# Delta rule of a two-block model: inverse as two 64x64 diagonal tiles per product, its levels in one stretch

## What is computed

```
decay = jnp.exp(jnp.where(causal, gc[..., :, None] - gc[..., None, :], -jnp.inf))
a_low = jnp.where(strict, jnp.einsum("bhnid,bhnjd->bhnij", k_beta, k) * decay, 0.0)
t_mat = a_low + jnp.eye(L, dtype=f32)
sol = lax.linalg.triangular_solve(t_mat, rhs, left_side=True, lower=True, unit_diagonal=True)
...
v_new = u_i - jnp.einsum("bhld,bhde->bhle", w_i, state)
```

## Time and profile before

| | us |
|---|---|
| median of 3 runs (917.66 to 919.14) | 919.08 |
| the profiled execution, its own time | 919.58 |
| its span, first to last instruction | 917.8 |
| TensorE busy | 904.7 |
| VectorE busy | 601.0 |
| ScalarE busy | 518.4 |

### The profile page before, as it was taken

One profiled execution on the slowest core, in us unless ns is written; L12 is line 12 of the kernel. 1 busy time (PEld: TensorE's weight loads), 2 busy tenths in 40 slices (PEclk: granted clock), 3 DMA queues, 4 the chain that ended last, 5 costly groups with the idle time before them and its releaser, 6 DMA issues.

```text
span 917.8 us, 16932 instructions
## 1 busy us (share of the span) xinstructions
PE 904.7 (99%) x6586; PEld 841.4 (92%) x6586; DVE 601.0 (65%) x959; ACT 518.4 (56%) x905; POOL 24.5 (3%) x36
## 2 busy tenths in 40 slices
PE   9999999999999999999999999999999999999998
PEld 7978899999998999999999999999987999999986
DVE  4689755555557666668786877755758455554576
ACT  6478754444446765567456464735549444444463
POOL 4100300000000000000000000000000000000000
PEclk9999999999999999999999999999999999999999
DMA  9814766665554455453222141415555555556541
GB/s 286 274 58 129 165 204 192 192 191 184 184 184 135 144 178 162 159 176 118 75 92 93 49 135 32 152 47 184 184 195 173 196 183 184 181 189 196 177 171 46
DMA packets 107647, 143.43 MB, mean 156 GB/s; under 512 B 3016, under 2 KB 95432, under 8 KB 107600
## 3 DMA queue, kind: packets, MB, share of 16 engines
q1 hardware_dynamic: 105648, 137.60, 46.6%
q0 software_dynamic: 1744, 4.98, 2.6%
q10 hardware_dynamic: 208, 0.20, 0.1%
HBM read 141.72 MB, written 1.05 MB: 156 GB/s over the span
## 4 chain that ended last, share of the span: by engine, by line
PE 82%; DVE 9%; ACT 5%; issue 3%; DMA 0%; DVEq 0%; ACTq 0%
PE ps L1762 15%; PE ps L1764 15%; PE ps L1763 15%; PE ps L1770 8%; PE ps L1768 8%; PE ps L1769 8%; PE ps L2170 2%; PE ps L2157 2%; PE ps L2174 2%; DVE R L1501 2%; DVE wl L1172 1%; ACT wh L627 1%; PE ps L1859 1%; PE ps L1841 1%; ACT R L951 1%
## 5 line engine op out<-in xcount | busy, mean ns | idle before, releaser
L1172 DVE TENSOR_TENSOR wl<-w_raw,wh 128x1024 fp32r<-128x1024 f32 x251 | 305.0, 1224 | 213.5 <-ACT wh L627 212.9
L1762 PE MATMUL ps<-xTh,wh 128*128 128x256 f32 (+1 forms) x1160 | 334.8, 289 | 0.9 <-DVE xTl L1198 0.8
L1763 PE MATMUL ps<-xTl,wh 128*128 128x256 f32 (+1 forms) x1160 | 326.2, 281 | 0.0
L1764 PE MATMUL ps<-xTh,wl 128*128 128x256 f32 (+1 forms) x1160 | 326.2, 281 | 0.0
L627 ACT ACTIVATE wh<-w_raw 128x1024 fp32r<-128x1024 f32 x251 | 263.1, 1053 | 81.5 <-PE ps L1770 60.2
L1762 PEld LDWEIGHTS ps<-xTh,wh 128*128 128x128 f32 x1160 | 219.1, 189 | 4.4 <-issue 2.7
L1763 PEld LDWEIGHTS ps<-xTl,wh 128*128 128x128 f32 x1160 | 218.4, 188 | 1.9 <-issue 1.0
L1764 PEld LDWEIGHTS ps<-xTh,wl 128*128 128x128 f32 x1160 | 219.2, 189 | 0.0
L1768 PE MATMUL ps<-wh,y 128*128 128x512 f32 x224 | 87.9, 392 | 0.0
L1770 PE MATMUL ps<-wh,y 128*128 128x512 f32 x224 | 87.6, 391 | 0.0
L1769 PE MATMUL ps<-wl,y 128*128 128x512 f32 x224 | 87.1, 389 | 0.0
(11 more groups left out here) (371 smaller groups left out, 1335.7 us busy)
## 6 DMA issues: line engine op xcount, KB each, us to landing
w_raw<-in_w_in_dram SPq DMA_DIRECT2D x42, 1024.0 KB, 5.2
w_raw<-in_w_ff_dram SPq DMA_DIRECT2D x32, 1024.0 KB, 5.5
w_raw<-in_w_ffn_gate_dram SPq DMA_DIRECT2D x11, 1024.0 KB, 5.3
w_raw<-in_w_ffn_up_dram SPq DMA_DIRECT2D x11, 1024.0 KB, 5.3
w_raw<-in_w_ffn_down_dram SPq DMA_DIRECT2D x11, 1024.0 KB, 4.9
w_raw<-in_w_out_dram SPq DMA_DIRECT2D x8, 1024.0 KB, 5.0
w_raw<-in_w_proj_a_dram SPq DMA_DIRECT2D x4, 1024.0 KB, 5.2
w_raw<-in_w_proj_b_dram SPq DMA_DIRECT2D x4, 1024.0 KB, 5.1
```

The source lines that it names most:

```text
L1172: TT(low_part, raw_unit(SLOT[p], j, layout), high_part.bitcast(F32), ALU.subtract).then_inc(w_lo, 1)
L1762: mm(out, wh_, xh, start=first, stop=False)
L1763: mm(out, wh_, xl, start=False, stop=False)
L1764: return mm(out, wl_, xh, start=False, stop=last)
```

## The change

**Compact form.** Levels 1 to 5 never leave the two diagonal blocks of 64 tokens, so `X_`, `XT_` and `PM_` are kept as 128 partitions x 64 columns (`Xc`, `XTc`, `PM_`), and each product of two 128x128 matrices becomes two products of 64x64, one on partitions 0 to 63 and one on 64 to 127. Level 6 is one 64x64 product per matrix in each of its two stages. The full `XT_` is put together afterwards by two ScalarE copies and one subtraction. The product for `X_` now goes to other PSUM banks (`fm`), with a semaphore of its own, and is issued after the one for `XT_` in each group. The transposition of `X_` is now made by 64x64 products with the identity, and VectorE copies it out (before: ScalarE).

**One stretch.** The levels stand in stages 6 to 17, with no steps between. `prepare`, `exponents`, `g_rows` come ahead of them, `out_transposes` behind, `out_root` in stage 3; `out_row` and `gate_rows` stay between the levels on VectorE. The silu of `zr` moves to the last stage. In stage 1 ScalarE's copy and split for unit 0 now both come after the norms.

**Besides.** The recurrent gate of the first block is computed with full 128x128 block-diagonal weights (before: two 64x64 halves each). The table of constants is smaller, some semaphores are merged, and TensorE's two middle rounds are written out (before: a loop).

```diff
-GDN_WEAVE = [9, 8, 4, 6, 4] + [1] * 12 + [4, 3, 3, 11]
+GDN_WEAVE = [2, 8, 4, 8, 7, 3] + [0] * 12 + [4, 3, 3, 22]
...
                         for j in range(2):
-                            last = mm(acc[:, 3 * g, j * P:(j + 1) * P], A_[:, 2 * g + j, :], XT_[:, 2 * g + j, :], start=True, stop=True)
+                            pr, out = 2 * g + j, acc[:, 3 * g, j * HB:(j + 1) * HB]
+                            if lv < 6:
+                                for part in blocks:
+                                    last = mm(out[part], A_[part, pr, part], XTc[part, pr, :], start=True, stop=True)
+                            else:
+                                last = mm(out[0:HB], A_[HB:P, pr, 0:HB], XTc[HB:P, pr, :], start=True, stop=True)
                         last.then_inc(lv_p[g], 1)
...
                         for j in range(2):
-                            pr = 2 * g + j
-                            last = mm(acc[:, 1 + g, j * P:(j + 1) * P], X_[:, pr, :], PM_[:, pr, :], start=True, stop=True)
+                            pr, out = 2 * g + j, acc[:, 1 + g, j * HB:(j + 1) * HB]
+                            for part in blocks[0:2 if lv < 6 else 1]:
+                                last = mm(out[part], Xc[part, pr, :], PM_[part, pr, :], start=True, stop=True)
+                        last.then_inc(lv_zt[g], 1)
...
                         if lv < 6:
                             for j in range(2):
-                                pr = 2 * g + j
-                                last = mm(acc[:, 1 + g, (2 + j) * P:(3 + j) * P], PM_[:, pr, :], X_[:, pr, :], start=True, stop=True)
-                        last.then_inc(lv_z[g], 1)
+                                pr, out = 2 * g + j, fm[:, g, j * HB:(j + 1) * HB]
+                                for part in blocks:
+                                    last = mm(out[part], PM_[part, pr, :], Xc[part, pr, :], start=True, stop=True)
+                            last.then_inc(lv_zx[g], 1)
...
-                for gate, w in ((fm[:, m % 2, 0:T1], wa_bd), (acc[:, m, 0:T1], wx_bd)):
-                    for half in (slice(0, 64), slice(64, 128)):
-                        last = mm(gate[half, :], w[half, m, half], xc[half, m, :], start=True, stop=True)
-                last.then_inc(r_ps, 1)
+                mm(fm[:, m % 2, 0:T1], wa_bd[:, m, :], xc[:, m, :], start=True, stop=True)
+                mm(acc[:, m, 0:T1], wx_bd[:, m, :], xc[:, m, :], start=True, stop=True).then_inc(r_ps, 1)
```

More of the change, by code:

```diff
@@ L69, in constant_table @@
     c[:, C_MLOW:C_LEV] = np.where(k < r, 0.0, NEG)
-    for n in range(LEVELS):
+    r64, k64 = np.arange(HB)[:, None], np.arange(HB)[None, :]
+    for n in range(LEVELS - 1):
         b = 1 << n
[L72 to L77, removed]
+        low = (r64 // (2 * b) == k64 // (2 * b)) & (r64 % (2 * b) >= b) & (k64 % (2 * b) < b)
+        c[:, level_mask(n)] = np.tile(low.T if n else low[:, 0::2], (2, 1))
+    c[:, C_ID2:C_MOBA] = np.tile(np.eye(HB, dtype=np.float32), (2, 1))
     diag = np.where(k <= r, 0.0, NEG)
@@ L960, in gdn_stage @@
                     ins.then_inc(kv_out, 1)
+                    if not (isinstance(a, int) and a == 0):
+                        out_root(a - 1)
                 if s == 4:
[L962 to L963 removed]
                     act.wait_ge(vT_ps, a + 1)
@@ L1023, in pair_round @@
                 before = ch.n
-                later = weave is GDN_WEAVE
                 for s, done in enumerate(finished(weave)):
                     stage(s, a)
-                    if later and s == 1:
-                        hi(fu + 4, 8, a)
                     for c in done:
-                        unit(c, fu + c, 8, a, pair, not (later and c == 0))
+                        unit(c, fu + c, 8, a, pair)
                 return ch.n - before if isinstance(ch.n, int) else None
@@ L1532, in gdn_stage @@
                     dve.wait_ge(inv_start, a + 1)
[L1533 to L1536, removed]
+                    low = PM_.rearrange("p r n -> p (r n)")[:, 0:4 * 32]
+                    first = cst[:, level_mask(0)].unsqueeze(1).to_broadcast([P, 4, 32])
+                    evens = A_.rearrange("p r (q two) -> p r q two", two=2)
+                    for b in range(2):
+                        part, qs = slice(HB * b, HB * b + HB), slice(32 * b, 32 * b + 32)
+                        ins = TT(rows4(low)[part], evens[part, :, qs, 0], first[part], ALU.mult)
+                    link(ins)
+                    grow(Xc, 0, 0, low.rearrange("p (m b) -> p m b", b=1)).then_inc(x0_out, 1)
                 if s == 4:
@@ L1545, in gdn_stage @@
                     prepare(a + 1)
-                if s == 10 and not (isinstance(a, int) and a == PAIRS - 1):
+                if s == 5 and not (isinstance(a, int) and a == PAIRS - 1):
                     exponents(a + 1)
-                if 5 <= s < 17 and s % 2 == 1:
-                    lv = (s - 5) // 2 + 1
+                if 6 <= s < 18 and s % 2 == 0:
+                    lv = (s - 6) // 2 + 1
+                    if lv == 1:
+                        for g in range(2):
+                            dve.wait_ge(xt0_ps, a * 2 + (g + 1))
+                            dve.tensor_copy(XTc[:, 2 * g:2 * g + 2, :], pairs(acc[:, 1 + 2 * g, 0:P])).then_inc(xt0_out, 1)
@@ L1557, in gdn_stage @@
+                    if not (isinstance(a, int) and a == 0):
+                        if 2 <= lv < 6:
+                            out_row(a - 1, lv - 2)
+                        elif lv == 6:
+                            gate_rows(a - 1)
+                if 6 <= s < 18 and s % 2 == 1:
+                    lv = (s - 6) // 2 + 1
                     for g in range(2):
-                        dve.wait_ge(lv_z[g], a * 6 + lv)
-                        z = acc[:, 1 + g, :].rearrange("p (r n) -> p r n", r=4)
@@ L1564, in gdn_stage @@
+                if s == 18 and not (isinstance(a, int) and a == 0):
+                    out_lo(a - 1)
+                if s == 18:
                     dve.wait_ge(uw_ps, a + 1)
@@ L1649, in _ @@
                 if m == 1:
-                    out_rows(3)
+                    for pr in range(4):
+                        out_row(3, pr)
+                    gate_rows(3)
                 if m == 4:
@@ L2133, in gdn_stage @@
                 if s == 4:
-                    pe.wait_ge(x0_out, a + 1)
-                    for pr in range(4):
-                        last = pe.transpose(acc[:, 3, pr * P:(pr + 1) * P], X_[:, pr, :], ident)
-                    last.then_inc(xt0_ps, 1)
                     pe.wait_ge(silu_v, a + 1)
@@ L2206, in gdn_stage @@
                     last.then_inc(o_ps, 1)
-                if s == 9 and not (isinstance(a, int) and a == PAIRS - 1):
-                    pe.wait_ge(tok_out, a + (PAIRS + 1))
-                    g_rows(a + 1)
-                if s == 13 and not (isinstance(a, int) and a == 0):
-                    pe.wait_ge(tok_out, a + (PAIRS + 1))
-                    pe.wait_ge(vb_out, a + 1)
-                    out_transposes(a - 1)
             def g_rows(b):
@@ L2251, in _ @@
             pair_round(GDN_WEAVE, gdn_stage, "fffffftt", G + 8, 0)
-            for i in rounds(pe, 2):
+            for i in range(2):
                 pair_round(GDN_WEAVE, gdn_stage, "fffffftt", G + 8, i + 1)
```

156 lines of the change are left out of this document (93 added, 63 removed).

## The result

The changed kernel takes **914.12 us** (median of 7 runs, 912.44 to 915.8) where the one before takes 919.17 beside it (7 runs, 917.66 to 919.76). The ratio is 0.9943, 95% interval 0.9932 to 0.9955, so it is faster by 0.6%. The profiled execution took 914.48 with a span of 912.7; before it was 919.58.

The account below looks back on a forecast made before the run. TensorE's work was taken to bound the kernel. Terms including -12.4 us (levels) and +9.8 (turn of a round) summed to -4.2: 915.4 in the profiled execution's time, so 914.9 us; range 908 to 928.

Parts of the forecast that it names:

- The pass: Spacing of 64-column passes on TensorE in the levels: 0.034 us taken, 0.028 if halves overlap, 0.066 as upper bound.
- A level: One of levels 1 to 5 of the inverse: 2.05 us, against 2.67 before without its steps.
- the first term: Levels 1 to 5 over four rounds: 20 x (2.05 - 2.67) = -12.4 us.
- Rival 3: TensorE-VectorE hand-overs in the levels priced too low eat the gain: about 918 to 920 us, chance 0.18.
- The turn: Before each round's sums of squares, seven steps no longer cover the wait for ScalarE: +2.46 x 4 = +9.8 us.
- Rival 2: The turn of a round costs nothing, something other than ScalarE's order sets the sums' start: 905.1 us, chance 0.08.
- rival 4: TensorE's clock falls to 1.2 GHz after each turn's 2.8 us wait: +14 us, so 929, chance 0.06.
- g_rows: Products ahead of the levels wait for prepare, late behind out_root: about 0.3 us in two rounds, +0.6 us.
- Entering and leaving the small form: Switching TensorE into and out of 64x64 products: about 0.1 us each time, +0.8 us in all.
- Level 6 and the transposition: The inverse's last level about 2.07 us, -1.4 in the sum; 16 small transposing passes plus VectorE's copy 0.91 us, +0.8.
- Recurrent gate: First block's gate: 16 full passes of 272 columns instead of 16 side-by-side pairs, 0 us.

Follow-up runs that it names:

- Experiment 4: Changed kernel with all 64x64 products of levels 1 to 5 on the upper half of the array, same number of instructions: 939.7 us, ratio 1.0234 to the kernel before.
- experiment 1: Kernel before with seven of nine weight steps ahead of the sums of squares put behind the round's last stage, unit 0's split at its usual place: 940.15 us.
- experiment 2: Changed kernel with nine weight steps ahead of the sums of squares again instead of two, ScalarE's split of unit 0 late again: 909.83 us.
- experiment 5: Changed kernel with eleven products of zeros put into TensorE's wait before the sums of squares of every round: 911.16 us.
- experiment 7: Changed kernel with ScalarE's out_root moved from stage 3 to stage 5, behind units 1 and 2: 915.16 us.
- experiment 6: Changed kernel with nine steps ahead of the sums, one weight step in each half level again, products for X in acc, unit 0's split late: 919.25 us.
- experiment 8: Kernel before with only the recurrent gate changed, to sixteen full 128x128 products instead of 32 of 64x64: 919.09 us, ratio 1.0002.

## Why the prediction was right, and where its terms were off

- **The pass, 0.034 taken, 0.028 to 0.066 as bounds.** Measured 0.029, at the low bound, in runs of 48. Experiment 4 shows the reason that the prediction gave for this bound, two halves at once; 0.058 on one half. My own choice between the bounds, from two loads 37 ns apart, was too high. The Trainium skill, "TensorE: Matmul & The Clock Gate", section "Back-to-back issue gap", was weighed with its 62 ns per matmul in software decode. The trace does not agree: the products start 29 ns apart in the mean. The 58 ns of experiment 4 lie near that figure, but they are what one half needs, and both halves together are twice as fast. The measurement decides.
- **A level, 2.05.** Measured 1.78, so the first term is 20 x (1.78 - 2.67) = -17.8 instead of -12.4. This is the mis-sized step. Of the 0.27 us, 39 x 0.005 = 0.20 are the pass. The rest is the hand-overs between TensorE and VectorE, for which some 0.07 too much was put in: the 0.06 from a load to its product and the 0.05 for a second semaphore had no row behind them, and the trace has load and product 0.01 apart (501.34 and 501.35). Rival 3, waits in the levels priced too low, had the sign wrong.
- **The turn, +9.8.** Right: 10.6 us of waits in four, 2.65 each, instead of 0.8 in all, behind ScalarE's squares (experiments 1 and 2). Rival 2 is out.
- **The clock (rival 4, 0.06).** The prediction had it at 1.00 and argued from the earlier trace rows that 4.6 idle us at the end left it alone. That step failed. Behind two of four turns it was at half, 3.2 us in the profiled execution, and experiment 5 shows the cause and gives 3.0 back. The rival's 14 us were too much: it is 1.5 to 1.7 each time, and not at every turn. The Trainium skill, same page, section "The HAM clock gate", has an idle engine fall to half clock. The trace agrees, and here waits of 2.6 us are enough, though not each time.
- **g_rows, +0.6.** Measured about 0.9 in each of two rounds, against 0.3: out_root stands ahead of unit 1's split (experiment 7), and VectorE sat idle 2.52 us before L1180. About +1.2 more.
- **Entering and leaving the small form, +0.1 each time.** This was too low as a price (experiment 6: 0.35 for the pair), but with one stretch a round it is paid only four times, so it moves the sum by 0.6 at most.
- **Level 6 and the transposition.** Level 6 takes 2.30 us in round 1 (507.62 to 509.92) for 2.07 forecast, the transposition 0.94 (497.80 to 498.74) for 0.91. Both near enough; they were not tested apart.
- **Recurrent gate, 0.** Right (experiment 8).

The sum in the profiled execution's time: -4.2 - 5.4 (levels) + 3.2 (clock) + 1.2 (`g_rows`) = -5.2, and measured is -5.1. That the forecast time of 914.9 came so close to 914.12 is luck in part: a gain and a loss that it did not have nearly cancel. What stays open: why the clock falls behind some of these equal waits and not behind others, what makes a full step among small passes dear, and 0.7 us of experiment 2.

## What to carry to other kernels

When work is taken from between dependent products to make one dense stretch, first ask which wait it covered elsewhere: here seven steps short at the turn cost 9.8 us of the 17.8 gained, and putting them back, with `out_root` later and work from behind the stretch moved ahead of it, gave another 13 us. A wait of TensorE of some 2.6 us costs more than its length, since the clock may fall behind it (1.4 to 1.7 us more here); and a second small gain can vanish in that until the wait is gone. Keep 64x64 products together: here, alternating them with full products cost about as much again as the full ones themselves (0.35 us for each step of 0.351).

## What the runs showed of the hardware

- 64-column float32 passes on the two 64x64 halves start every 0.058 us on each half, both halves at once, 0.029 in the mean. The order in which the two halves' passes are issued, four by four or two by two, makes no difference (1.82 and 1.78 a level).
- A three-product step of 128x128 between such passes costs 0.70 us instead of 0.351, without any wait on a semaphore (experiment 6).
- The granted clock went to 1.2 GHz behind 12 of 20 waits of TensorE of 2.6 to 2.8 us, over the traces of five kernels, and cost 1.4 to 1.7 us each time. Where steps or products of zeros filled these waits it stayed at 2.4 GHz, at 28 of 28 turns. Behind a wait of 2.5 us at `g_rows` it fell in one of four cases (experiments 2 and 6).
